# Query blocks routed two heads at a time, and six modulation rows multiplied behind gate slabs

## The reference

```python
q = xn @ peer_wq                        # 256 x 2048: per head two halves of 128
s0, s1 = q_half0 @ subkeys[0].T, q_half1 @ subkeys[1].T      # 128 scores each
i0, i1 = top16(s0), top16(s1)           # per token, head and half
pairs  = s0[i0][:, None] + s1[i1][None, :]                   # 16 x 16
best   = top16(pairs)                   # expert number = 128 * i0 + i1
gate   = softmax(best over 16)
act    = gelu(xn . peer_u[expert])      # 8 * 16 = 128 dot products a token
out    = sum(gate * act * peer_v[expert])
```

## Time and profile before

| | us |
|---|---|
| median of 3 runs | 3932.86 (3928.84 to 3938.31) |
| profiled execution | 3935.61 |
| span of its trace | 3933.9 |
| query projection (PE) | 641 to 729 |
| transposes and scores | 730 to 745 |
| routing of tile 0 (DVE) | 746 to 800 |
| dots, sums of tile 0 | 810 to 1162, 1162 to 1511 |
| dots, sums of tile 1 | 1511 to 1851, 1851 to 2198 |
| dilated block ends, gated linear block starts | 2757, 2759 |
| level loop | 2783 to 2872 |

### The profile page before, as it was taken

How to read it: one execution, slowest core, us unless ns; L and a number is a source line. 1 busy time by engine, 2 the same in 40 slices (tenths; PEclk the granted TensorE clock), 3 DMA queues, 4 the chain that set the end, 5 groups by cost and what they waited for, 6 DMA issues and landing times. The chain is left out here.

```text
span 3933.9 us, 28544 instructions
## 1 busy us (share of the span) xinstructions
PE 2324.2 (59%) x10328; PEld 1723.1 (44%) x10328; DVE 2544.3 (65%) x2372; ACT 798.8 (20%) x670; POOL 1272.3 (32%) x705
## 2 busy tenths in 40 slices
PE   7799988710000000000000599988889989999999
PEld 4333556400000000000000488877668868888787
DVE  3544544679999989998888644366855644444444
ACT  1000233200000000000000233234333333333333
POOL 2531000057878888888888200000000000000000
PEclk9899989855555555555555799989999989999999
DMA  6588465699999999999999555433345645555554
GB/s 195 197 312 293 177 217 199 220 410 406 400 387 387 392 371 388 407 402 399 382 378 396 210 193 192 160 118 123 122 171 198 245 138 184 191 192 187 176 192 161
DMA packets 332244, 1029.47 MB, mean 262 GB/s; under 512 B 35256, under 2 KB 35768, under 8 KB 264696
## 3 DMA queue, kind: packets, MB, share of 16 engines
q1 hardware_dynamic: 258424, 491.31, 36.1%
q0 software_dynamic: 73728, 536.90, 33.9%
HBM read 1021.28 MB, written 6.86 MB: 261 GB/s over the span
## 5 line engine op out<-in xcount | busy, mean ns | idle before, releaser
L357 DVE TENSOR_TENSOR slab_low<-ring,slab_high 128x2048 fp32r<-128x2048 f32 x240 | 549.7, 2292 | 691.9 <-ACT slab_high L350 691.8
L350 ACT CAST slab_high<-ring 128x2048 fp32r<-128x2048 f32 x304 | 579.7, 1909 | 1038.0 <-PE bank L336 791.9
L1844 PE MATMUL bank<-ident,nat 128*128 128x128 f32 x32 | 8.9, 433 | 1290.6 <-DVE nat L1700 1290.6
L1655 DVE SCALAR_TENSOR_TENSOR res<-pool,res 128x2048 f32<-128x2048 f32 x256 | 603.1, 2356 | 75.3 <-DMA pool<-in_peer_v,small 43.6
L334 PE MATMUL bank<-slab_high,left_high 128*128 128x512 f32 x1568 | 616.7, 393 | 23.4 <-DVE slab_low L357 20.4
L335 PE MATMUL bank<-slab_low,left_high 128*128 128x512 f32 x1568 | 614.2, 392 | 0.0
L336 PE MATMUL bank<-slab_high,left_low 128*128 128x512 f32 x1568 | 614.0, 392 | 0.0
L1641 DVE CUSTOM_DVE_ANT_0 pool<-pool,nat 128x2048 f32<-128x2048 f32 x256 | 575.9, 2291 | 58.7 <-DMA pool<-in_peer_u,small 47.9
L1794 POOL DMA_INDIRECT pool<-in_peer_v,small x256 | 545.3, 2130 | 102.5 <-issue 68.3
L1844 PEld LDWEIGHTS bank<-ident,nat 128*128 128x128 f32 x32 | 5.7, 217 | 1294.3 <-DVE nat L1700 1294.3
L1794 POOL DMA_INDIRECT pool<-in_peer_u,small x256 | 504.6, 1971 | 143.3 <-issue 73.0
(11 more groups left out here) (525 smaller groups left out, 2574.4 us busy)
## 6 DMA issues: line engine op xcount, KB each, us to landing
ring<-in_w_in SPq DMA_DIRECT2D x148, 1024.0 KB, 4.8
ring<-in_w_ada SPq DMA_DIRECT2D x96, 1024.0 KB, 7.2
ring<-in_w_ffn_in SPq DMA_DIRECT2D x88, 1024.0 KB, 4.8
ring<-in_w_ffn_out SPq DMA_DIRECT2D x44, 1024.0 KB, 5.0
ring<-in_w_out SPq DMA_DIRECT2D x32, 1024.0 KB, 5.8
ring<-in_peer_wq SPq DMA_DIRECT2D x16, 1024.0 KB, 5.9
ring<-in_w_br_gla SPq DMA_DIRECT2D x8, 1024.0 KB
gate_rows<-slab_low_scratch SPq DMA_DIRECT2D x9, 512.0 KB, 5.8
```

The costliest lines, as they stand in the source:

```text
L350: nc.scalar.copy(high[:, n % PARTS], ring[:, g % SLOTS]).then_inc(high_done, 1)
L357: eng.tensor_tensor(dst, ring[:, g % SLOTS], high[:, n % PARTS].bitcast(F32), ALU.subtract)\
L1655: v.scalar_tensor_tensor(res[:, t, :], rows_[r], actv[:, t, bass.ds(i * GB + r, 1)], res[:, t, :], ALU.mult, ALU.add).then_inc(s_free, 1)
```

## The change

**Queries.** `project_rows` and the block of transposes and scores become one block. The queries go through four blocks of 512 columns, two heads each. PE transposes the queries of block b after the first slab of block b + 1, and multiplies its scores after the second. DVE routes blocks 0 and 1 for tile 0, two heads (32 experts) at a time, between the low casts of blocks 2 and 3; blocks 2 and 3 are routed between the first dots. POOL starts with the first gathers as soon as the experts of block 0 are known, with five row buffers (`EARLY`) until the other three, which hold scores and queries, are free. The 24 slabs of the last six modulation rows are no longer there. `best_keys`, `best_pairs` and the rest take the heads as an argument.

**Late slabs.** The 24 slabs go into the list of the gates, two behind each of G21 to G32 (`late_slabs`, called from `gate_slabs`). They use PSUM bank 5. Their left operand (`spread`, 0.5 MB) is kept in DRAM and read back. Behind the last of them DVE copies the bank, PE adds the four groups of 32 rows, DVE adds the bias and SP writes the six rows to DRAM.

```diff
-        ROWS_ROUTE = ROWS - FIRST_NORM2 - ROWS_NORM2
+        FIRST_LATE = FIRST_NORM2 + ROWS_NORM2
+        ROWS_LATE, LATE_EACH, LATE_GATE, LEVEL_GATE = ROWS - FIRST_LATE, 2, 21, 24
+        LATE_GATES = 4 * ROWS_LATE // LATE_EACH
+        assert LATE_EACH * LATE_GATES == 4 * ROWS_LATE
...
+        def late_before(n):
+            return LATE_EACH * min(LATE_GATES, max(0, n - LATE_GATE))
+        def gate_and_late(n, s):
+            for m in range(3 * 4 * OB):
+                at_ = m + late_before(m)
+                if n == at_:
+                    return gates(m // 4, m % 4)
+                if at_ < n < m + 1 + late_before(m + 1):
+                    x = 4 * FIRST_LATE + late_before(m) + n - at_ - 1
+                    return [(0, KS, cols(w_ada, KS * (x % 4), x // 4 * NB))]
...
-            Section(ROWS_ROUTE, 4, plain(w_ada, (ROWS - ROWS_ROUTE) * NB)),
             Section(C_A // NB, 4, plain(w_in2)),
-            Section(3 * OB, 4, gates),
+            Section(3 * 4 * OB + 4 * ROWS_LATE, 1, gate_and_late),
...
-        project_rows("peer_q", PEER_Q, lambda t, b: q_nat[:, t, b * NB:(b + 1) * NB], peer_small)
...
+        EARLY = 5
+        QB = PH * 2 * HALF // NB
+        QH, QG = PH // QB, NB // KEYS
+        borrowed = Places(pool, EARLY * D)
+        sk_nat, skT = borrowed.take(2, HALF), borrowed.take(2, KEYS)
+        cand_first, hot_first = borrowed.take(QH, TOPK * TOPK), borrowed.take(QH * TOPK, TOPK)
+        borrowed = Places(pool, (EARLY + 1) * D)
+        first_scores = borrowed.take(2, TT, QG, KEYS)
+        borrowed = Places(pool, (EARLY + 2) * D)
+        q_blk, qT = borrowed.take(TT, NB), borrowed.take(KS, T)
...
+                def keys_of_block(b):
+                    dve.wait_ge(s_scc, b + 1)
+                    best_keys(0, 0, block_heads(b))
+                    next_keys(0, block_heads(b))
+                    best_keys(0, 1, block_heads(b))
+                def first_dots(lo, hi):
+                    for r in range(lo, hi):
+                        buf = rows_[r % EARLY]
+                        dve.wait_ge(s_row[r], 16)
+                        v.tensor_tensor_reduce(out=buf, in0=buf, in1=nat[:, 0, :], scale=1.0, scalar=0.0, op0=ALU.mult,
+                                               op1=ALU.add, accum_out=dots[:, r:r + 1]).then_inc(s_free, 1)
+                    if hi == GB:
+                        dve.wait_ge(s_free, GB)
+                        v.tensor_copy(actv[:, 0, 0:GB], dots).then_inc(s_dv, 1)
+                        dve.wait_ge(s_dv, 1)
...
+                for m in range(2 * KS):
+                    low_part(dve, gq + m)
+                    if m == KS - 1:
+                        dve.wait_ge(s_skT, 1)
+                        v.tensor_copy(skT, view(ps[7][:, 0:2 * P], [2, P])).then_inc(s_skc, 1)
+                dve.wait_ge(s_io, 1)
+                for b in range(2):
+                    hb, m = block_heads(b), gq + KS * (b + 2)
+                    keys_of_block(b)
+                    low_part(dve, m)
+                    best_pairs(0, hb)
+                    low_part(dve, m + 1)
+                    best_pairs(1, hb)
+                    low_part(dve, m + 2)
+                    key_numbers(hb)
+                    chosen_key(0, hb)
+                    if b == 0:
+                        chosen_key(1, hb)
+                        experts(0, hb)
+                    low_part(dve, m + 3)
+                chosen_key(1, hb)
+                experts(0, hb)
+                first_dots(0, GB)
+                hb = block_heads(2)
+                dots_of(0, 1, 2)
+                keys_of_block(2)
+                dots_of(0, 2, 3)
+                best_pairs(0, hb)
+                best_pairs(1, hb)
+                dots_of(0, 3, 4)
+                key_numbers(hb)
+                chosen_key(0, hb)
+                chosen_key(1, hb)
+                experts(0, hb)
+                hb = block_heads(3)
+                dots_of(0, 4, 5)
+                keys_of_block(3)
+                dots_of(0, 5, 6)
+                best_pairs(0, hb)
+                best_pairs(1, hb)
+                dots_of(0, 6, 7)
+                gate_differences(0)
+                key_numbers(hb)
+                chosen_key(0, hb)
+                chosen_key(1, hb)
+                experts(0, hb)
+                dots_of(0, 7, 8)
                 softmax(0)
-                dots_of(0, 0, 2)
-                best_keys(1, 0)
-                dots_of(0, 2, 4)
-                dve.wait_ge(slabs_used, first_slab[ADA_R + 1])
-                v.tensor_tensor(mod_acc, mod_acc, ps[0][:, :], ALU.add).then_inc(s_mtk, 1)
-                next_keys(1)
-                dots_of(0, 4, 7)
+                best_keys(1, 0, every)
+                dots_of(0, 8, 9)
+                next_keys(1, every)
+                dots_of(0, 9, 11)
                 dve.wait_ge(s_mb, 16)
                 dve.wait_ge(s_msum, 1)
-                v.tensor_tensor(mod_b[0:ROWS, :], mod_b[0:ROWS, :], ps[1][0:ROWS, :], ALU.add).then_inc(s_mba, 1)
-                best_keys(1, 1)
-                dots_of(0, 7, 10)
-                best_pairs(0)
-                dots_of(0, 10, 13)
-                best_pairs(1)
-                dots_of(0, 13, HB)
+                v.tensor_tensor(mod_b[0:FIRST_LATE, :], mod_b[0:FIRST_LATE, :], ps[3][0:FIRST_LATE, :], ALU.add).then_inc(s_mba, 1)
+                best_keys(1, 1, every)
+                dots_of(0, 11, 13)
+                best_pairs(0, every)
+                dots_of(0, 13, 14)
+                best_pairs(1, every)
+                dots_of(0, 14, HB)
...
+                def first_halves():
+                    for p in range(2):
+                        st = stage[:, p * GB:(p + 1) * GB]
+                        g.tensor_copy(st, idx[:, 0, p * GB:(p + 1) * GB]).then_inc(s_stage, 1)
+                        g.wait_ge(s_stage, p + 1)
+                        for r in range(GB):
+                            if p == 0 and r >= EARLY:
+                                g.wait_ge(s_free, r - EARLY + 1)
+                            if p == 1 and r < GB - EARLY:
+                                g.wait_ge(s_free, EARLY + r + 1)
+                            if p == 1 and r == EARLY:
+                                g.wait_ge(s_idx, 2)
+                                g.wait_ge(s_sc, QB)
+                                g.wait_ge(s_kept, 1)
+                            gather(a["peer_u"][0], r, rows_[r % EARLY if p == 0 else r], st)
...
+                per = HB // 2 // QB
+                for b in range(QB):
+                    g.wait_ge(s_idx, b + 1)
+                    if b == 0:
+                        first_halves()
+                    halves(0, max(1, per * b), per * b + per)
...
+                sp.dma_start(sk_nat, a["peer_subkeys"][0].rearrange("h k d -> k h d")).then_inc(s_sk, 16)
+                stream(sp, PEER_Q)
+                sp.dma_start(spread_kept.rearrange("p (k n) -> p k n", k=KD), spread).then_inc(s_mtk, 16)
+                sp.wait_ge(s_mtk, 16)
+                sp.wait_ge(slabs_used, first_slab[MIX])
+                sp.dma_start(mod_b[0:FIRST_LATE, :], bias_rows[0:FIRST_LATE]).then_inc(s_mb, 16)
...
+                        if j == 0 and b >= 2:
+                            pe.wait_ge(s_q, 2 * (b - 1))
+                        slab(pe, gq + KS * b + j, [(ps[2 * (b % 2) + t][:, :], t) for t in range(TT)], left, KS * j,
+                             j == 0, j == KS - 1)
+                        if b == 0 and j == 1:
+                            pe.wait_ge(s_sk, 16)
+                            for i in range(2):
+                                last = nc.tensor.transpose(ps[7][:, i * P:(i + 1) * P], sk_nat[:, i, :], ident[:, :])
+                            last.then_inc(s_skT, 1)
+                        if b and j == 0:
+                            query_transposes(b - 1)
+                        if b and j == 1:
+                            block_scores(b - 1)
+                query_transposes(QB - 1)
+                block_scores(QB - 1)
...
+                for m in range(KS * QB):
+                    b, j = divmod(m, KS)
+                    high_part(act, gq + m)
+                    if b and j == 1:
+                        take_queries(b - 1)
+                    if b and j == 2:
+                        copy_queries(b - 1)
+                    if 0 < b < QB - 1 and j == 3:
+                        copy_scores(b - 1)
+                take_queries(QB - 1)
+                copy_scores(QB - 2)
+                nc.scalar.copy(scores[:, 1, 0:2 * QG, :].rearrange("p (b g) k -> p b (g k)", b=2),
+                               first_scores[:, :, 1].rearrange("p b g k -> p b (g k)")).then_inc(s_kept, 1)
+                copy_queries(QB - 1)
+                copy_scores(QB - 1)
...
+                if LATE_GATE <= n < LATE_GATE + LATE_GATES:
+                    late_slabs(pe, n - LATE_GATE)
...
+        def late_slabs(pe, i):
+            pe.wait_ge(s_ll, 32)
```

(48 more changed lines are left out.)

297 lines of the change are left out of this document (139 added, 158 removed).

## The result

The changed kernel takes 3950.97 us at the median (3936.32 to 3961.8), the kernel before 3936.01 (3928.84 to 3940.61), 13 runs each: ratio 1.0038, 95% interval 1.0027 to 1.0048. A second set of runs gave 1.0038 too (1.0024 to 1.0052). So it is slower by some 15 us, where the sum gave 3933.6, no change (with a chance of 0.42; over all cases 0.37 stood for faster, 0.30 for the same and 0.33 for slower); the time lies within the range of 3903 to 3965.

What follows compares the result with a forecast made beforehand. PE was taken to bound the query projection, DVE routing, tile 0's dots and gated levels, transfers the other gather stages. Profiled 3935.6 - 57.8 + 58.5 = 3936.3, less 2.7 to the median: 3933.6 us, range 3903 to 3965.

Steps and rivals of the forecast that it cites:

- Start of the dots: First dot product after routing by blocks: expected at 730.4, 79.5 us earlier than 809.87.
- The dots of tile 0: Stage of tile 0's dots: bound by DVE, with 8 us of waits for rows, ending at 1103.8 instead of 1161.6.
- Part A: Query projection, routing and first dots: gathers start earlier, -57.8 us in all.
- The levels: Gated linear part: two levels take 29.0 us, not 20.6, through late gate loads; +33.6 in eight levels.
- The boundary: Ahead of the gated block: G22's load is issued only when G20 is used, the barrier waits for its cast; +4.9.
- G21 to G24: Gates where PE has little room: eight late slabs cost 8.5 us and the lower clock 0.9; +9.4.
- The tail: Behind G32: two late slabs, the copy of the sum and PE's four additions delay awaited products; +4.2.
- Part B: Late slabs behind the gates: levels, clock, boundary, G21 to G24 and tail together, +58.5 us.
- Part B hides: Rival in the gated part: loads come early enough, levels keep 10.28 us, only 12.7 stays; 3887.8, chance 0.10.
- Loads land as if alone: Rival in the levels: the third load lands in 4.8 us, two levels take 25.9; 3921, chance 0.13.
- The lower clock holds: Rival on PE from G25 to G32: gate slabs take 10.2 us at the lower clock, +19; 3953, chance 0.15.
- the 6.4 in the sum: Levels on PE: the lower clock behind longer gaps adds 1.6 us to one gate slab per two levels, four times.

Runs made afterwards that it cites:

- own slots, later: Changed kernel with two slots outside the ring for late slabs, pairs behind G23 to G34, sum taken off the tail's queues: 3898.7 us, 0.9895 of the kernel before.
- slots of its own: Changed kernel with the same 24 late slabs loaded into two slots outside the ring: 3907.4 us against 3933.0 for the kernel before, ratio 0.9936.
- the filler: Changed kernel with ten products of 128 x 512 into an unused bank ahead of each gate slab of the levels: ratio 1.0039 to the kernel before.

## Why the prediction was right, and where it was off

- **Start of the dots.** 730.4 predicted, 729.36 measured, though of the 80.5 us some 3 come from a difference ahead of the stage.
- **The dots of tile 0.** DVE-bound with 8 us of waits, end at 1103.8 predicted; 1103.9 measured, 8.0 us of waits. Part A: -57.8 predicted, -57.7 at that point and -56.5 at 2400, 56 by the medians of the kernel without late slabs. The mechanism held; that the figures agree to 0.1 us is luck, since the second profile has -54.1 and -44.7 at the same places.
- **But its composition was told wrong.** The text said that the modulation slabs beside the routing bind nothing. Taking them away alone gave 17.5 us at the end of that stage and 10 at 2200. The sum came out right all the same, because it was made from DVE's work without the old waits. Kept beside the new dots, they cost 30 us: the two parts help each other, and the gain of the first half isn't the routing's alone.
- **The levels.** Two levels 29.0, plus 1.6 for the clock, predicted; 31.1 in the pair shown, and term by term: gate slab with the lower clock 7.1 predicted and 7.2 measured, late slabs 2.3 and 2.0, landing 7.9 and 8.5, cast and exponential 3.0 and 3.0, DVE's chain 10.3 and 10.4. From G24 to G32 the gated part grows by 43.2 (5.7 in the first level, 37.5 in seven) where 40.0 stood.
- **The boundary.** 4.9 predicted for the load of G22. The rows below (SP's issue, ACT's cast, and PE's first instruction behind the barrier) give 2702.95 to 2707.86, 4.9. The offset grows by 4.8 there and by 3.7 more up to the point where G21 and its late slabs are done. Of these 3.7, the two late slabs themselves are 1.9 (they stood under the 9.4). Not in the sum was what follows a PE idle for 7.14 us: the block starts at the lower clock (0.58 for two transposes, 0.38 before), and G21 takes 7.4 us where 5.7 is the full clock.

```profile
2702.95 0.37 SPq L297 DMA_DIRECT2D ring<-in_w_in  x1
2707.86 1.90 ACT L374 CAST slab_high<-ring 128x2048 fp32r<-128x2048 f32 x1 [10.58 <-DMA ring<-in_w_in]
...
2710.07 0.58 PE L2668 MATMUL bank<-ident,small 128*16 128x128 f32 x2 [7.14 <-PEq L2354]
```

- **G21 to G24.** 9.4 predicted for PE's time over four gates; 10.8 measured over G22 and G23, and 12.7 with G21's late slabs. It is more, and for another reason. ACT's cast of G23 stands 19.56 us for its load, with the exponential and logarithm of the gates queued behind it: the load chain binds there already.

```profile
2729.32 1.90 ACT L374 CAST slab_high<-ring 128x2048 fp32r<-128x2048 f32 x1 [19.56 <-DMA ring<-in_w_in]
```

- **The tail.** 4.2 predicted, 7.7 measured: the additions took 3.62 where 1.1 stood.
- **The sum.** Part B 58.5 predicted; 4.8 + 3.7 + 10.8 + 43.2 + 7.7 = 70.2 measured. These 12 us are two thirds of the error of 17: with -57.8 they give 3945.3. Of the rest to 3951, 3.1 is how the kernel before itself came out (3936.0 by 13 runs, not 3932.9 by three), and 2.6 is within the spread of the runs.
- **The rivals.** "Part B hides" needed another ring, and with one (own slots, later) 15.1 us is what stays, near the 12.7 it named. "Loads land as if alone" fell: 8.5 and 9.6 us. "The lower clock holds" named +19 and 3953, which is where the time ended, but it wanted gate slabs of 10.2 us and none took more than 8.6: the right number from the wrong place.

The Trainium skill (TensorE: Matmul & The Clock Gate, "HAM oscillation — how this bites in real kernels") describes products that start again at the lower clock after each wait for a DMA. The trace agrees: G25 and G27 begin with 0.80 us for a first product that takes 0.50 at full clock, and the levels have 0.84 where the kernel with slots of its own has 1.00. But the length of the one idle gap ahead does not tell which slabs are hit: G25 had stood 2.19 us (with 3.54 before the products of the level ahead of it), and in the kernel before a slab behind 2.73 us began at full clock. As for the 6.4 in the sum: G25, G27, G29 and G31, the chain that it counts, took 7.2, 7.1, 7.1 and 8.5 us on PE, 7 more together than at 5.7 each. By the rows the term is about right; the filler could neither confirm it nor refute it.

## What to carry to other kernels

A slab put into a shared ring can cost far more by its place there than by its time on the engine (here some 5 to 7 of 70 us): count, for each slab that others wait on, which use frees its slot and what is queued ahead of its load, before looking at who is idle. Work that seems free beside a serial stretch may hold up the first transfers of the next one; leave it out in one run before moving it. And where two parts of a change meet in one resource, measure each alone: here 11 or 25 us for the first half with the slabs kept, 10 to 14 for taking them away, and some 56 for both.

## What the runs showed of the hardware

- Three loads of 1 MB in a burst: the third lands 8.5 us after its issue when issued 1.9 us behind the first, 9.6 when about 1.0 behind, and 10.2 in one burst with a write behind it; a lone one takes 4.8.
- Beside gathers at a DMA share of 0.92, 24 MB more cost 30 us, 1.25 us for each; gathers and loads together then move 399 GB/s, as the gathers alone did in the kernel before (400).
- Four additions of 128 x 512 in float32 over 32 columns of the identity take 3.62 us on PE at full clock (eight instructions), where the eight of a modulation slab take 1.06. The four products of a slab go to four different groups of 32 rows of the bank, the additions all to the same one; that this is the reason wasn't tried.
